# Three edits to a two-layer encoder kernel: early low halves, whole transpose groups, and a (3, 2) projection quota for one tile

## The chip, the cores and the metric

One core of one Trainium2 chip. The time is device microseconds (us) of one execution; lower is better. The kernel is one launch and runs both layers one after the other.

## The reference, cut to what matters

Each of two layers computes `x <- x + RMSNorm(W_out . [A, B, C])` for 1024 prompt rows and 64 sample rows that share the weights. All three branches read `RMSNorm(x)` through one input projection:

```python
proj = einsum('bld,de->ble', rmsnorm(x), w_in)
# A: 4-tap causal convolution, gates, linear recurrence
# B: index scores relu(q_idx . k_idx) summed over 8 heads, top 256 keys per query,
#    softmax over the selected keys only, times v, 4 heads
# C: two softmax maps per head, p0 - lam * p1, times v, RMSNorm per head, 4 heads
mix = einsum('ble,ed->bld', concat([y_a, y_b, y_c]), w_out)
x = x + rmsnorm(mix, norm_post)
```

Attention is block-causal, so a later tile of 128 prompt rows sees more keys. The sample rows see 1024 cached keys and their own 64.

## The kernel before, in words

Rows are split into nine tiles: 0 to 7 are prompt tiles of 128 rows, tile 8 (`SAMPLE`) holds the 64 sample rows. A layer has a **front** and an **attention part**, each written out as a list of steps that every engine walks in the same order, each picking its own steps.

The front (`front()`, L235) begins with transposes of x on TensorE (PE, L1772), and with the index query projection "iq": two halves by three pieces of tokens, six pieces of eight float32 matmuls (L1810; each such matmul is two instructions). Its order is iq pieces, index keys "ik" (L1796), further projections, then the index scores (L1847), with other projections between them, the gates of branch A and the value rows. The projection pieces go around a ring of four PSUM banks. An iq bank is free once ScalarE (ACT) has copied the high half out (L1184, semaphore `high_ready`) and VectorE (DVE) has taken the rounded-off low half, PSUM minus high (L1491, `ring_drained`). DVE walks its own program in order: scale and drain the x tiles (L1432, L1453), then some 20 tiny operations for lambda and the decay constants (L1457 to L1474), then the high and low halves of the cached index keys (L1478, L1480), and then, in a loop over eight ring pieces (L1485), the low halves of iq and ik. Later DVE searches the 256th score of each row by bisection (L1556) and writes the selection masks (L1672 to L1675); only then does it take part in attention.

The attention part (`schedule()`, L145) has 68 **units**, one head (two heads for tile 8) of one tile, in tile order 7, 8, 6, 0, 1, 2, 3, 4, 5. Place n of this order is the number in the steps `("proj", n, q)` and `("rows", n)`. A tile has its C units first (two softmax maps) and then its B units (one map, keys selected). Unit numbers used below: tile 7 is 0 to 7, tile 8 is 8 and 9 (C), 10 and 11 (B), tile 6 is 12 to 19, tile 3 is 44 to 51 (its B, "selected", units 48 to 51), tile 4 is 52 to 59 (C 52 to 55), tile 5 is 60 to 67. In each unit i the list holds: the scores of unit i+1 (`qk`, L1979), DVE's maximum (L1690), ACT's exponential (`exp`, L1344), the combination of the two maps for C (`comb`, L693 to L701), transposes of the map in groups of four 128-key blocks (`tr`, L2010), their evacuation to SBUF (DVE for B, ACT for C: L678, L680), the product with the values of unit i-1 (`pv`, L2032) and its division (`div`, L717 to L731).

All transpose groups share one PSUM bank (`tbank`): PE starts a group only when the one before is evacuated. The 1088 keys of tile 8 make three groups, the third with 64 keys only. The list carries a remainder `rest` for it: the third group of a tile 8 unit is emitted in the following unit, behind that unit's first scores.

Between these steps lies the output projection of a finished tile: `ytr` (L2042) transposes its 512 attention columns, ACT copies them (L1360), and 16 `proj` steps follow (L2077, two instructions each; 8 steps for tile 8). `QUOTA` (L91) says how many a unit of a tile takes, as (C unit, B unit). The last step is followed by ACT's sum of squares (`square`, L1403) and `rows` (DVE L1728 scales the product out of PSUM, GpSimd L1125 adds x, SyncE stores). Places 5 and 6 (tiles 2 and 3) and 7 (tile 4) use the same PSUM banks, so the first `proj` of one waits for the `rows` of the one before. `take()` (L163) holds the next tile's projection back by one unit for that. What is left at the last unit is done behind it, in front of the last tile's own 16 steps.

Of the kernel before, what the change touches and what calls it, by code (L numbers as in the profile page):

```python
# [6 lines left out]
P = 128  # L7
# [16 lines left out]
HI, DI = 8, 32  # L24
# [36 lines left out]
TOKENS = [(0, 384), (384, 384), (768, 320)]  # L61
# [26 lines left out]


FIRST_PROJ = 0  # L90
QUOTA = {0: (2, 3), 1: (2, 2), 2: (2, 2), 3: (3, 3), 4: (2, 2), 5: (2, 2), 6: (2, 1)}  # L91
YTR = 2
NARROW_MIX = (1, 3)
LATE, NEXT_LATE = ORDER[-1], ORDER[-2]
EARLY_X = [[0, 1, 2], [t for t in range(3, NT) if t not in ORDER[-2:]]]
NARROW_END = 7
FIRST_X = 3
ROWS_AT = {-1: [("tm", "bv", 2), ("tm", "bv", 3)], 0: [("tm", "bv", 4)], 1: [("tm", "bv", 5), ("tm", "bv", 6)]}
LAST_ROWS = sum(ROWS_AT.values(), [])

# [44 lines left out]
def schedule():  # L145

    units = ATT
    steps = []
    waiting = []
    finish = []  # L150
    hold = [FIRST[ORDER.index(SAMPLE) + 1] + FIRST_PROJ]
    begun = [0]
    rest = []

    def scores(i):

        if not begun[0] <= i < len(units):
            return []
        begun[0] = i + 1
        return [[("qk", i, m)] + ([("qk2", i, m)] if units[i][0] == SAMPLE else []) + [("exp", i, m)]  # L160
                for m in range(maps_of(i))]

    def take(i, most):  # L163

        new = []
        while waiting and most and i >= hold[0]:
            n, q = waiting.pop(0)
            new.append(("proj", n, q))
            most -= 1
            if q == proj_steps(ORDER[n]) - 1:  # L170
                new.append(("square", n))
                late = 2 if mix_place(n + 1) == mix_place(n) else 1
                finish.append((i + 1, n))
                if late == 2:
                    hold[0] = i + 2
        return new

    steps += sum(scores(0), []) + ROWS_AT[-1]
    for i, (t, kind, h) in enumerate(units):
        nk = -(-width(t) // P)  # L180
        groups = [("tr", i, g) for g in range(-(-nk // 4))]
        rows_now = [("rows", finish.pop(0)[1])] if finish and finish[0][0] <= i else []
        quota = QUOTA.get(t, (0, 0))["CB".index(kind)]
        pv = [("pv", i - 1)] if i else []
        div = [("div", i - 1)] if i else []
        n = NTH[i]
        ytr = []
        if i - FIRST[n] == YTR + 1 and n:
            ytr = [("ytr", n - 1)]
            waiting += [(n - 1, q) for q in range(proj_steps(ORDER[n - 1]))]  # L190
        nxt = scores(i + 1)
        one, two = (nxt + [[], []])[:2]
        own = [("comb", i)]
        plain = kind == "B"
        if len(groups) == 1:
            head = one[:-1] + ytr + one[-1:] + own if plain else own + one[:-1] + ytr + one[-1:]
            soon = rows_now if width(t) > 2 * P else []
            steps += head + take(i, 1) + pv + soon + two + take(i, quota - 1) + groups + div
            steps += [] if soon else rows_now
        elif t == SAMPLE and kind == "C":  # L200
            ahead = scores(i + 2)[0] if len(nxt) == 1 and maps_of(i + 2) == 1 else []
            steps += own + one[:-1] + two[:-1] + rest + ytr + groups[:1] + rows_now + one[-1:] + two[-1:]
            if ahead:
                steps += ahead[:-1] + groups[1:2] + pv + groups[2:] + div + ahead[-1:]
                rest = []
            else:
                steps += pv + groups[1:2] + div
                rest = groups[2:]
        elif t == SAMPLE:
            steps += one[:-1] + rest + ytr + one[-1:] + own + rows_now + two[:-1]  # L210
            steps += groups[:1] + two[-1:] + pv + groups[1:2] + div
            rest = groups[2:]
        elif plain:
            steps += one[:-1] + ytr + one[-1:] + own + take(i, 1) + groups[:1] + two
            steps += take(i, quota - 1) + pv + div + groups[1:] + rows_now
        else:
            steps += own + one[:-1] + rest + ytr + two[:-1] + take(i, 1) + groups[:1] + rows_now + one[-1:] + two[-1:]
            steps += ROWS_AT.get(i, [])
            rest = []
            steps += take(i, quota - 1) + pv + div + groups[1:]  # L220
    last = len(units)
    hold[0] = last
    steps += [("pv", last - 1), ("div", last - 1)]
    while len(waiting) > 2:
        hold[0] = last
        steps += take(last, len(waiting) - 2)
    steps += [("ytr", NT - 1)] + take(last, 2) + [("rows", n) for _, n in finish]
    waiting += [(NT - 1, q) for q in range(proj_steps(ORDER[-1]))]
    hold[0] = last
    new = take(last, 2 * KT)  # L230
    steps += new + [("rows", NT - 1)]
    return steps
# [109 lines left out]
def build(nc, x0, w_in, acst, gate_w, npost, w_out, ckT, kidxT, vcache,  # L342
# [7 lines left out]
    with ctx:  # L350
# [270 lines left out]
        def on_ring(key, w=BANK, r=P):  # L621
            b = RINGBANK[key]
            return ps[0:r, BANK * b:BANK * b + w]
# [7 lines left out]
        def drains_ring(ins, key):  # L631
            return ins.then_inc(ring_drained[RINGBANK[key]], 1)
# [101 lines left out]
        for layer in range(DEPTH):  # L734
# [5 lines left out]
            with nc.Block() as block:  # L740
# [666 lines left out]
                def _(dve):  # L1407
                    steps = [0]

                    def link(ins):  # L1410
                        steps[0] += 1
                        ins.then_inc(dve_step, 1)
                        dve.wait_ge(dve_step, steps[0])
# [23 lines left out]
                    for t in range(NT):  # L1437
# [16 lines left out]
                        if not has_prev and 3 <= t + 1 < NT:  # L1454
                            scale_x(t + 1, t + 2, xt[t + 1])

                    dve.wait_ge(lam_e, 1)  # L1457
                    link(vec.tensor_tensor(lamp, lams[:, 3:4], lams[:, 2:3], ALU.subtract))
                    vec.tensor_tensor(nlam, lamp, cst[:, C_INIT:C_INIT + 1], ALU.subtract).then_inc(lam_ready, 1)
# [20 lines left out]
                    vec.tensor_tensor(ikcs[half, :], ikc[half, :], ikcs[half, :].bitcast(f32), ALU.subtract)\  # L1480
                       .then_inc(kc_low, 1)

                    third = slice(64, 96)
                    n = 0
                    for key in list(RINGJOB)[:2 * len(TOKENS) + 2]:  # L1485
                        _, u, c, p = key
                        n += 1
                        dve.wait_ge(high_ready, n)
                        if u == "iq":
                            c0, cn = TOKENS[p]  # L1490
                            drains_ring(vec.tensor_tensor(iq3[1][:, c, c0:c0 + cn], on_ring(key, cn),  # L1491
                                                          iq3[0][:, c, c0:c0 + cn].bitcast(f32), ALU.subtract), key)
                        else:
                            cols = slice(2 * IKW * p, 2 * IKW * (p + 1))
                            vec.tensor_copy(iks[DI:2 * DI, cols], iks[0:DI, cols].bitcast(f32))
                            link(vec.tensor_tensor(iks[third, cols], ikf[0:DI, cols], iks[0:DI, cols].bitcast(f32),
                                                   ALU.subtract))
                            vec.tensor_copy(iks[96:P, cols], iks[third, cols].bitcast(f32)).then_inc(kn_low, 1)

                    for j in range(AJ):  # L1500
                        vec.memset(ax[j][:, 0:3], 0.0)
# [671 lines left out]
```

## Time and profile before

| what | value |
|---|---|
| three runs | 1584.02, 1585.23, 1580.79 us (median 1584.02) |
| the profiled execution | 1586.94 us |
| its span, first to last instruction | 1585.2 us |
| mean granted TensorE clock | 0.987 |
| PE busy | 1523.2 us (96%) |
| DVE busy | 1140.4 us (72%) |
| ACT busy | 648.3 us (41%) |
| GpSimd (POOL) busy | 371.5 us (23%) |

PE is TensorE's matmul side. "Idle before" is the time for which an engine had nothing to execute before an instruction, with the instruction that ended the wait. A granted clock of 1.00 is TensorE's 2.4 GHz level, 0.50 its 1.2 GHz level; a window's figure is the mean over it. Layer 0 runs to about 793.5 us of the span, layer 1 from there.

### The profile page before, as it was taken

To read this page: it belongs to the slowest core of one execution; us is meant where nothing else is said; L and a number is where in the kernel's file an instruction comes from. 1 tells how busy PE (TensorE), PEld (TensorE's weight loads), DVE (VectorE), ACT (ScalarE), POOL (GpSimd) and SP (SyncE) were. 2 spreads that over 40 slices of the span, in tenths; PEclk is the share of its full clock that TensorE was granted. 3 is DMA by queue.
4 is the path that set the end of the run, shared out by engine and by line. 5 is a ranking of instruction groups with operands and counts; after the bars stand their busy time and mean duration, and the time that the engine had idled before them with its cause. 6 is when DMAs were issued, how large, how long until landed. Compare 5 with 4: busy or idle time off the path is not lost. (4 is left out here: it accounts for less than half of the span.)

```text
span 1585.2 us, 21171 instructions
## 1 busy us (share of the span) xinstructions
PE 1523.2 (96%) x7264; PEld 1026.0 (65%) x7286; DVE 1140.4 (72%) x2482; ACT 648.3 (41%) x1270; POOL 371.5 (23%) x461
## 2 busy tenths in 40 slices
PE   7999999999999899999989999999999999999997
PEld 5566556678877665566556665566788766556664
DVE  5479979998966556666443799899989666565662
ACT  3385760219143333434314757402371433343341
POOL 2000341430001244332310004404200121434221
PEclk9999999999999999999999999999999999999999
DMA  5101001231015112120411200023210341112111
GB/s 189 57 13 42 27 27 27 79 99 49 27 50 207 67 34 67 43 68 11 170 60 57 27 27 27 27 50 97 80 54 1 116 144 66 51 56 68 41 35 40
DMA packets 73114, 98.16 MB, mean 62 GB/s; under 512 B 42736, under 2 KB 61680, under 8 KB 68656
## 3 DMA queue, kind: packets, MB, share of 16 engines
q1 hardware_dynamic: 73008, 96.80, 19.9%
q8 instruction: 59, 0.97, 0.2%
q14 instruction: 47, 0.39, 0.1%
HBM read 65.79 MB, written 18.14 MB: 53 GB/s over the span
## 5 line engine op out<-in xcount | busy, mean ns | idle before, releaser
L1810 PE MATMUL ps<-r_xn,r_w 128*128 128x384 f32 (+1 forms) x1728 | 563.7, 476 | 7.8 <-DVE r_xn L1453 2.7
L1810 PEld LDWEIGHTS ps<-r_xn,r_w 128*128 128x128 f32 x1728 | 325.5, 192 | 198.4 <-issue 24.9
L1556 DVE TENSOR_SCALAR_CACHE_REDUCE r_ix<-r_sc,smi 128x768 bf16<-128x768 f32 (+6 forms) x380 | 342.1, 963 | 2.2
L1344 ACT ACTIVATE r_sc<-ps,sm 128x1024 f32<-128x1024 f32 (+8 forms) x204 | 155.5, 765 | 225.8 <-DVE sm L1690 225.6
L1896 PE MATMUL ps<-r_w,r_xn 128*128 128x256 f32 x1024 | 224.0, 380 | 0.0
L1896 PEld LDWEIGHTS ps<-r_w,r_xn 128*128 128x128 f32 x1024 | 193.8, 190 | 26.8 <-issue 1.0
L1690 DVE TENSOR_REDUCE sm<-ps 128x1 f32<-128x1024 f32 (+8 forms) x204 | 156.2, 786 | 54.5 <-PE ps L1985 20.5
L2032 PEld LDWEIGHTS ps<-r_vg,r_w 128*128 128x128 f32 (+1 forms) x1168 | 147.6, 192 | 53.1 <-issue 33.5
L2032 PE MATMUL ps<-r_vg,r_w 128*128 128x64 f32 (+1 forms) x1168 | 148.3, 271 | 1.3 <-DVE r_w L678 1.2
L2077 PE MATMUL ps<-r_xn,r_ag 128*128 128x512 f32 x256 | 134.2, 623 | 2.6 <-ACT r_vg L1360 2.6
L2077 PE MATMUL ps<-r_xn,r_vg 128*128 128x512 f32 x256 | 131.0, 607 | 0.4 <-DMA r_xn<-w_out 0.2
L2010 PEld LDWEIGHTS ps<-ident,r_sc 128*128 128x128 f32 (+1 forms) x648 | 80.7, 147 | 73.2 <-issue 55.4
L2010 PE MATMUL ps<-ident,r_sc 128*128 128x128 f32 (+1 forms) x648 | 110.6, 281 | 11.2 <-DVE r_w L680 5.3
L1518 DVE SCALAR_TENSOR_TENSOR r_sc<-r_vg,sm,r_sc 128x384 f32<-128x384 f32 (+6 forms) x98 | 97.8, 998 | 27.2 <-ACT r_vg L1252 21.6
L678 DVE COPY r_w<-ps 128x512 f32<-128x512 f32 (+3 forms) x104 | 59.1, 568 | 80.1 <-issue 51.8
L1252 ACT ACTIVATE r_vg<-ps 128x384 f32<-128x384 f32 (+6 forms) x112 | 88.4, 795 | 28.5 <-PE ps L1847 22.7
L678 ACT COPY r_w<-ps 128x512 f32<-128x512 f32 (+3 forms) x104 | 50.6, 486 | 115.4 <-PE ps L2010 114.7
L717 DVE TENSOR_SCALAR r_q<-ps,sm 128x64 f32<-128x64 f32 x128 | 35.9, 281 | 82.0 <-PE ps L2032 81.5
L1306 ACT ACTIVATE r_ix<-r_sc,smi 128x896 bf16<-128x896 f32 (+2 forms) x60 | 67.2, 1120 | 24.5 <-DVE smi L1654 17.4
L700 DVE SCALAR_TENSOR_TENSOR r_sc<-r_sc,sm 128x512 f32<-128x512 f32 (+3 forms) x104 | 67.9, 682 | 2.4
L1847 PE MATMUL ps<-iks,iqs 128*128 128x384 f32 (+3 forms) x160 | 67.7, 494 | 1.5 <-ACT iqs L1234 1.5
L1058 POOL CAST qb_hi<-r_qk 64x256 fp32r<-64x256 f32 x32 | 12.6, 394 | 239.5 <-ACT r_vg L1294 232.6
(256 smaller groups left out, 1868.9 us busy)
## 6 DMA issues: line engine op xcount, KB each, us to landing
r_w<-w_in SPq DMA_DIRECT2D x24, 1024.0 KB, 5.0
r_xn<-w_out SPq DMA_DIRECT2D x4, 2048.0 KB, 7.5
y<-r_res SPq DMA_DIRECT2D x15, 512.0 KB, 2.9
r_vg<-x SPq DMA_DIRECT2D x8, 512.0 KB, 8.6
r_w<-w_in SPq DMA_DIRECT2D x16, 256.0 KB, 5.5
r_xn<-vcache SPq DMA_DIRECT2D x2, 2048.0 KB, 12.5
o_v<-r_vg SPq DMA_DIRECT2D x4, 1024.0 KB, 10.6
r_sc<-x SPq DMA_DIRECT2D x8, 512.0 KB, 4.6
```

The lines of the kernel that those rows point to most:

```text
L678: ins = copy(pT[i % 2][:, k0:k1, 0:r], src[:, 0:k1 - k0, 0:r])
L700: vec.scalar_tensor_tensor(e0, e1, cf, e0, ALU.mult, ALU.add).then_inc(comb_ready, 1)
L1252: drains_x(nc.scalar.activation(dst, src, ACT.Relu, scale=scale), key)
L1344: ins = nc.scalar.activation(ex[2 * (i % 2) + m][0:r, 0:w], on_slot(("qk", i, m), w, r), ACT.Exp, bias=negm[0:r, c:c + 1], accum_out=den[0 ...
L1518: ins = vec.scalar_tensor_tensor(sc[t][0:r, 0:w], src, iw[0:r, t, h:h + 1], sc[t][0:r, 0:w], ALU.mult, ALU.add)
L1556: ins = vec.tensor_scalar(unsel[t][0:rows(t), :], sc[t][0:rows(t), :], b, None, op, ALU.add, accum_out=cnt[0:rows(t), c:c + 1])
L1690: vec.tensor_reduce(negm[0:r, c:c + 1], on_slot(s, w, r), X, ALU.max, negate=True)\
L1810: ins = nc.tensor.matmul(on_ring(key, cn), w[:, k, P * s:P * (s + 1)], xnT[:, k, c0:c0 + cn], start=(k == 0), stop=(k == KT - 1))
L1896: ins = nc.tensor.matmul(on_ring(key)[:, BW * (t - t0):BW * (t - t0 + 1)], xnT[:, k, P * t:P * (t + 1)], w[:, k, :], start=(k == 0), stop= ...
L2010: ins = nc.tensor.transpose(tbank[0:kn, P * (k - 4 * g):P * (k - 4 * g) + r], ex[2 * (i % 2)][0:r, P * k:P * k + kn], ident[0:r, 0:r])
L2032: ins = nc.tensor.matmul(obank[0:r, 0:vals.shape[1]], pT[i % 2][0:kn, k, 0:r], vals, start=(k == 0), stop=(k == nk - 1))
L2077: ins = nc.tensor.matmul(mixb[:, half, :], yk, wo[:, k, BANK * half:BANK * (half + 1)], start=(k == 0), stop=(k == KT - 1))
```

## The change: what it does

Three edits, in both layers.

1. `QUOTA` of tile 3 goes from (3, 3) to (3, 2): its four B units take two projection steps each in place of three.
2. Tile 8's units no longer leave their third transpose group to the next unit if they are B units: all groups of the unit stand in it. New branches for scores two units ahead and for an early start are added to the same place.
3. DVE takes the first four low halves (`EARLY_LOWS = 4`, the iq pieces of the first two token pieces) directly behind the last x tile, before the tiny operations and the cached keys; the other four stay where all eight were.

```diff
-QUOTA = {0: (2, 3), 1: (2, 2), 2: (2, 2), 3: (3, 3), 4: (2, 2), 5: (2, 2), 6: (2, 1)}
+QUOTA = {0: (2, 3), 1: (2, 2), 2: (2, 2), 3: (3, 2), 4: (2, 2), 5: (2, 2), 6: (2, 1)}
+EARLY_LOWS = 4
         elif t == SAMPLE:
-            steps += one[:-1] + rest + ytr + one[-1:] + own + rows_now + two[:-1]
-            steps += groups[:1] + two[-1:] + pv + groups[1:2] + div
-            rest = groups[2:]
+            ahead = []
+            if i + 2 < len(units) and maps_of(i + 1) == maps_of(i + 2) == 1:
+                ahead = scores(i + 2)[0]
+            early = i == FIRST[n]
+            steps += one[:-1] + ytr + ([] if early else one[-1:]) + own + rows_now + two[:-1]
+            if ahead and len(ahead) == 3:
+                steps += groups[:1] + (one[-1:] if early else []) + ahead[:1] + groups[1:2] + ahead[1:2] + groups[2:] + pv + ahead[2:] + div
+            elif ahead:
+                steps += groups[:1] + ahead[:1] + groups[1:2] + pv + groups[2:] + ahead[1:] + div
+            else:
+                steps += groups[:1] + two[-1:] + pv + groups[1:] + div
         else:
-            steps += own + one[:-1] + rest + ytr + two[:-1] + take(i, 1) + groups[:1] + rows_now + one[-1:] + two[-1:]
+            steps += own + one[:-1] + ytr + two[:-1] + take(i, 1) + groups[:1] + rows_now + one[-1:] + two[-1:]
...
+                    def lows(first, last):
+                        for n in range(first, last):
+                            key = list(RINGJOB)[n]
+                            dve.wait_ge(high_ready, n + 1)
...
+                    lows(0, EARLY_LOWS)
                     dve.wait_ge(lam_e, 1)
...
-                    for key in list(RINGJOB)[:2 * len(TOKENS) + 2]:
...
+                    lows(EARLY_LOWS, 2 * len(TOKENS) + 2)
```

The lists that come out, for PE, around tile 8's B units (10 and 11) and tile 6's first unit, layer by layer the same:

```
before: tr10.0 pv9 tr10.1 | qk12.0 tr10.2 ytr0 qk12.1 tr11.0 pv10 tr11.1 | qk13 tr11.2 proj0.0 tr12.0 proj0.1 pv11
after:  tr10.0 pv9 tr10.1 tr10.2 | qk12.0 ytr0 qk12.1 tr11.0 pv10 tr11.1 tr11.2 | qk13 proj0.0 tr12.0 proj0.1 pv11
```

The projection of tile 2 (place 5) ended in unit 53 and ends in unit 55; `rows5` stood in unit 54 and stands in unit 56. Tile 3's (place 6) covered units 55 to 62 and covers 57 to 64; `rows6` moves from unit 63 to 65. Tile 4's (place 7) had 8 of its 16 steps in units 64 to 67 and now has 4 in units 66 and 67; 12 in place of 8 steps are left behind unit 67.

## Rows read from the trace of the kernel before

**Rows 1.** The page: its first line.

```profile
span 1585.2 us, 21171 instructions
```

**Rows 2.** Waits of PE: releaser, us in total, times, longest.

```profile
PE ps L2010 <- DVE r_w L680: 5.3, 2, 2.7
PE ps L2042 <- DVE r_w L680: 4.2, 2, 2.1
...
PE ps L1810 <- issue: 2.6, 1, 2.6
...
PE ps L1810 <- DVE iq_lo L1491: 2.6, 1, 2.6
```

**Rows 3.** Timeline, front of layer 0: start, us, engine, line, instruction, idle before.

```profile
39.05 0.15 DVE L1458 TENSOR_TENSOR sm<-sm 128x1 f32<-128x1 f32 x1
...
42.51 0.49 ACT L1184 ACTIVATE iq_hi<-ps 128x384 fp32r<-128x384 f32 x1 [5.51 <-PE ps L1810]
...
44.41 1.95 DVE L1491 TENSOR_TENSOR iq_lo<-ps,iq_hi 128x384 fp32r<-128x384 f32 x4
```

**Rows 4.** Windows: bounds, length, PE busy, granted clock, DMA share, GB/s.

```profile
42.00:52.00 10.00, 7.40 (x22) 0.83 0.00 0
827.00:837.00 10.00, 7.45 (x22) 0.83 0.00 0
516.00:536.00 20.00, 15.26 (x82) 0.83 0.06 14
1302.00:1322.00 20.00, 16.70 (x87) 0.83 0.14 35
704.00:714.00 10.00, 8.37 (x36) 0.83 0.36 121
1486.00:1498.00 12.00, 10.01 (x45) 0.72 0.31 102
470.00:480.00 10.00, 8.75 (x63) 1.00 1.00 303
```

**Rows 5.** Timeline, PE at the B units of tile 8, layer 0.

```profile
514.11 0.66 PE L2010 MATMUL ps<-ident,r_sc 128*128 128x128 f32 x4
...
518.12 0.66 PE L2042 MATMUL ps<-ident,r_q 128*128 128x128 f32 x4 [2.09 <-DVE r_w L680]
...
529.62 1.02 PE L2010 MATMUL ps<-ident,r_sc 128*128 128x128 f32 x4 [2.65 <-DVE r_w L680]
```

**Rows 6.** Timeline, DVE at the same place.

```profile
514.80 0.69 DVE L678 COPY r_w<-ps 128x512 f32<-128x512 f32 x1 [1.89 <-PE ps L2010]
...
517.79 0.27 DVE L680 COPY r_w<-ps 64x128 f32<-64x128 f32 x1
```

**Rows 7.** Timeline, DVE and PE at tile 4, units 54 and 55, layer 0.

```profile
703.52 1.27 DVE L1728 SCALAR_TENSOR_TENSOR r_res<-ps,sm,r_ix 128x1024 f32<-128x1024 f32 x1
...
701.83 0.63 PE L2010 MATMUL ps<-ident,r_sc 128*128 128x128 f32 x4 [0.38 <-DVE r_sc L700]
...
704.85 0.47 PE L1979 MATMUL ps<-kst_b,qb_hi 128*128 128x512 f32 x1 [1.21 <-DVE r_res L1728]
...
707.25 2.04 PE L2077 MATMUL ps<-r_xn,r_ag 128*128 128x512 f32 x2 [0.78 <-ACT r_vg L1360]
```

**Rows 8.** Timeline, PE at unit 63, layer 0.

```profile
748.94 0.66 PE L2010 MATMUL ps<-ident,r_sc 128*128 128x128 f32 x4 [0.69 <-ACT r_vg L1360]
```

**Rows 9.** Timeline, DVE and PE in a B unit of tile 4.

```profile
712.26 0.48 PE L1979 MATMUL ps<-kst_b,qb_hi 128*128 128x512 f32 x1
...
713.48 0.82 DVE L1690 TENSOR_REDUCE sm<-ps 128x1 f32<-128x640 f32 x1 [0.50 <-PE ps L1985]
...
716.60 0.48 PE L1979 MATMUL ps<-kst_b,qb_hi 128*128 128x512 f32 x1
```

**Rows 10.** The chain that ended last, behind unit 67 of layer 1: start, us, what.

```profile
1562.04 15.47 PE ps L2077 x36
```

**Rows 11.** Timeline, DVE's first instruction of the attention part, layer 0.

```profile
445.02 1.23 DVE L1690 TENSOR_REDUCE sm<-ps 128x1 f32<-128x1024 f32 x1 [1.54 <-PE ps L1992]
```

More of the change, by code:

```diff
@@ L216, in schedule @@
         else:
-            steps += own + one[:-1] + rest + ytr + two[:-1] + take(i, 1) + groups[:1] + rows_now + one[-1:] + two[-1:]
+            steps += own + one[:-1] + ytr + two[:-1] + take(i, 1) + groups[:1] + rows_now + one[-1:] + two[-1:]
             steps += ROWS_AT.get(i, [])
-            rest = []
             steps += take(i, quota - 1) + pv + div + groups[1:]
@@ L1455, in _ @@
                             scale_x(t + 1, t + 2, xt[t + 1])
+                    third = slice(64, 96)
+                    def lows(first, last):
+                        for n in range(first, last):
+                            key = list(RINGJOB)[n]
+                            _, u, c, p = key
+                            dve.wait_ge(high_ready, n + 1)
+                            if u == "iq":
+                                c0, cn = TOKENS[p]
+                                drains_ring(vec.tensor_tensor(iq3[1][:, c, c0:c0 + cn], on_ring(key, cn),
+                                                              iq3[0][:, c, c0:c0 + cn].bitcast(f32), ALU.subtract), key)
+                            else:
+                                cols = slice(2 * IKW * p, 2 * IKW * (p + 1))
+                                vec.tensor_copy(iks[DI:2 * DI, cols], iks[0:DI, cols].bitcast(f32))
+                                link(vec.tensor_tensor(iks[third, cols], ikf[0:DI, cols], iks[0:DI, cols].bitcast(f32),
+                                                       ALU.subtract))
+                                vec.tensor_copy(iks[96:P, cols], iks[third, cols].bitcast(f32)).then_inc(kn_low, 1)
+                    lows(0, EARLY_LOWS)
                     dve.wait_ge(lam_e, 1)
@@ L1481, in _ @@
                        .then_inc(kc_low, 1)
-                    third = slice(64, 96)
-                    n = 0
-                    for key in list(RINGJOB)[:2 * len(TOKENS) + 2]:
[L1486 to L1498, printed above, removed]
+                    lows(EARLY_LOWS, 2 * len(TOKENS) + 2)
                     for j in range(AJ):
```

## The prediction

> **What bounds the kernel now.** I read the page first, then PE's waits, then the timeline around each long wait, then windows of the granted clock. The profiled execution took 1586.94 us, its span 1585.2 [rows 1]; so it stands 2.9 us above the median of the runs, 1584.02, and 1.7 us lie around the span. What I take off is taken off both alike. PE is busy for 1523.2 us of the span, no other engine beyond 1140.4; PE is the bound, and its time can only fall where it waits or where its clock is at the lower level. The waits of PE [rows 2] show few long ones: 2.6 us in each layer in front of the third iq piece pair (L1810), 2.1 and 2.65 us in each layer at L2042 and L2010, all behind DVE. A last group stands at tile 4 [rows 7]: 0.38, 1.21 and 0.78 us within 6 us. The reader should then see in the windows [rows 4] that each of these places also has a granted clock below 1: 0.83 over 10 us is 1.7 us of clock time lost, and each such window starts with one of these waits. So a wait costs its length and, at five places in layer 0 and its twins in layer 1, some 1.7 us more.
>
> **Early low halves.** DVE ends the x tiles at 39.05 and goes through the tiny operations and the cached keys until 44.41; only then it frees the first ring bank (L1491, 0.49 us each), while PE stood from 42.47, for 2.6 us [rows 2, 3]. After the change three of the four high halves are there at 39.05, so the first bank is free at 39.6, 2.9 us before PE asks. The fourth low half needs ACT's copy that ends at 43.0 [rows 3]; DVE waits for it, and its 5.3 us of other work moves to 43.5 to 48.9. Who waits for that: the index scores, which need the cached keys at 68; and the ring bank of the fifth piece, whose high half came at 51.3 even before. Cost zero, covered by two whole iq pieces; without the cover it would be 5.3 us. Gain: 2.60 + 2.55 us of wait, and the clock at 42 to 52 and 827 to 837, 0.17 x 10 us each [rows 4]: 3.4. **Sum 8.55.** Bounds: 5.15 if the clock falls nevertheless, 8.55 if not.
>
> Does that reach the end? PE's front leads to DVE's search. DVE begins attention after a wait of 1.54 us for PE [rows 11]; its search starts from the index scores and moves with them. PE itself waits for DVE nowhere there. I let it pass whole.
>
> **Whole groups in tile 8's B units.** No instruction is added; the third group and its evacuation (0.27 us) move. The new branches never run with this tile order: they ask for two more one-map units behind, and unit 12 has two maps. Before, `ytr0` came right behind the third group, whose evacuation stood in DVE's queue behind the division of unit 9 and a maximum, at 517.79 [rows 6]: a wait of 2.09 [rows 5]. The second time the evacuation stood behind a division, a combination and a maximum: 2.65. After: the third group follows the second with only that one's evacuation between. The second ends at 514.77, its evacuation at 515.49 [rows 5, 6]: a wait of 0.75 to 0.8, once in unit 10 and once in unit 11. `ytr0` then has unit 12's scores in front and finds the bank empty. `tr12.0` waits for the combination, which now comes behind a small evacuation and a division only: by DVE's durations about 4.1 us behind the end of pv10, where PE arrives at 3.7; I take 0.5. New waits per layer 0.8 + 0.8 + 0.5 = 2.1 against 4.74: 2.6 gained. On clock, the windows 516 to 536 and 1302 to 1322 lose 0.17 x 20 = 3.4 us each [rows 4]. Waits of 0.34 and 0.91 us within 3 us left the clock at 1.00 in the window from 470 to 480; the new ones are smaller or further apart, so I take all of it back. **Sum 2 x (2.6 + 3.4) = 12.0.** Bounds: the clock stays lost, 5.2; the waits vanish, 16.2. Two edges lose something: DVE's maxima come 0.5 us later, still ahead of pv11; and the second half of w_out is fetched behind unit 11's product, so it moves with it.
>
> Transposes themselves run at both levels here: four take 0.66 us at 514.11 and 1.02 at 529.62, behind the long wait [rows 5]. The Trainium skill has a rule that speaks against this part: its page "TensorE: Matmul & The Clock Gate", section "Part 4: PE-mode transpose", says that the full clock "doesn't engage" for transposes. By it, two groups in a row with a wait between them would bring the low level back at these four places, and the sum here would be 5.2. The 0.66 speaks against the rule as it stands; whether the clock falls sooner among transposes the trace does not separate.
>
> **The quota of tile 3.** A step is two instructions of 0.43 us [rows 10], 0.86. Four units give up one each; tile 2's last three groups of two now lie in units 53 to 55, and 4 steps more, 3.4 us, stand behind unit 67. PE's work is the same; the sum is waits and clock. Removed per layer: in unit 54 two steps go between the scores and `tr54.0` and cover the 0.38 and most of the 1.21 (DVE and ACT need 4.5 us for such a unit, PE with two steps 4.7); in unit 55 a step covers ACT's copy of `ytr6`, 0.78 [rows 7]; in unit 63 the same, 0.69 [rows 8]. 3.06 us. Clock: 1.7 at 704 to 714, and 0.28 x 12 = 3.4 at 1486 to 1498, where 0.4 of it lies on a wait already counted [rows 4]: 4.7.
>
> Added: units 56 and 65 have no steps. A B unit of tile 4 takes 4.34 us with two steps [rows 9], so 2.6 without. DVE needs, from its start, 1.2 until the scores are there, 0.82 for the maximum, 0.69 for the first evacuation, some 1.1 for division and second evacuation, and then `rows5`, 1.27 [rows 7, 9]: 5.1. The second group waits 0.35 for the first evacuation, and proj6.0, due at 2.6 + 0.35 + 1.0 of scores, waits for `rows5` 1.05. At unit 65 the same gives about 0.2 and 0.8. Together 2.4 per layer. Zero if PE's stream is slower than I lay it out; 3.5 if GpSimd's root comes late. POOL's addition of `rows5` comes behind its head norm, later by some 4 us; its readers, the store and `rows6`, are 30 us away. SyncE's queue has `rows5` now behind tile 5's query copies instead of before; both are early. Tile 3's own units stay PE's: with two steps they hold 3.7 us against less than 2 of DVE. In layer 0 the longer remainder moves the last tile's chain together with the steps behind it. **Sum 6.1 + 4.7 - 4.8 = 6.0.**
>
> Total 8.55 + 12.0 + 6.0 = 26.5. I take off 1 for edges (unit 54's 0.15, unit 10's division later by 0.6). So 25.5: 1561.4 for the profiled execution, and **1558.5** against the median.
>
> **Rivals.**
>
> A. *The new waits lower the clock.* Places: tile 8's four (two in each layer) and units 56/57, 65/66 in both layers, eight in all, 1.7 us each. For: 1.21 and 0.78 us sufficed in layer 0, and in layer 1 the level was low already right behind the 1.21 [rows 4, 7]; units 56/57 have 1.4 us of waits in 2 us. Against: 470 to 480. With half of the eight, +6.8: 1565. (The Trainium skill's rule on transposes, above, would give it at the tile 8 places.)
> B. *DVE takes the front's gain back.* If the search does not move with PE, PE may gain only the 1.54 us [rows 11] of the 4.3 a layer: +5.5, 1564. Against: every wait of DVE in the front is for ACT, POOL or PE, which all move.
> C. *Slower.* TensorE falls to 1.2 GHz at every wait left or new in tiles 8, 6, 4 and 5, ten a layer or more. Price 1.7 us each; it turns the result from the 15th place on (25.5 / 1.7), and 20 would give 1592. Against: ten waits of 0.3 to 0.5 us leave 1.00 now.
> D. *The part on tile 3 does nothing*, its waits for `rows` being as long as the ones removed: 1564.5; it is a case of A by size.
>
> **How the numbers follow.** Forecast as laid out: 0.60, with 1554 to 1562 of its own (the added waits of tile 4 vanish, -4.8; one or two falls of the clock, +3.4). A 0.23, B 0.06, D 0.06, C 0.02, and 0.03 for no change by something unseen. The range runs from 1553 to 1570: it holds A to seven places, B and D. About 0.3% (4.8 us) is what a measurement of this kernel can tell from no change. Faster by more 0.95, within 0.03, slower 0.02.
>
> **What would show it.** The waits of L1810 for `iq_lo` and of L2042 and L2010 for L680 gone; in tile 8 two waits of L2010 for L678 of 0.8 us in each layer; windows at the five places at 1.00; units 54 and 55 without 1.21 and 0.78; two new waits of L2077 for DVE's L1728, near 1.0 and 0.8 us; a remainder behind unit 67 longer by 3.4 us. I am wrong if the clock is low at tile 8 still, if PE meets DVE where attention begins, or if L2077 waits for L1728 for over 2 us.

## The result, and the profile after

The changed kernel took **1560.19 us** in the median of four executions (1555.93 to 1562.50), the kernel before 1583.86 beside it on the same chip (1580.79 to 1585.23): a ratio of **0.985**, 95% interval 0.9825 to 0.9876. The prediction was 1558.5 with a range of 1553 to 1570, so the size came out. Whether the reasons did is what the rest is about: one of its two kinds of gain was too large, the other too small.

The page of the profiled execution (1560.33 us; mean granted clock 0.997, before 0.987), its span and each engine's busy time with its share of the span:

```profile
span 1558.5 us, 21195 instructions
PE 1510.0 (97%) x7286; PEld 1017.4 (65%) x7286; DVE 1132.5 (73%) x2482; ACT 649.5 (42%) x1270; POOL 370.7 (24%) x461
```

The span is 26.7 us shorter than in [rows 1]. PE's idle times, summed over its timeline, fell from 52.1 to 38.8 us; PE's busy time fell by 13.2 (from 1523.2), although its instructions are the same. That second half is clock: the same matmuls took less time at the higher level. The line numbers of the kernel have moved: L1810 is now L1823, L2010 L2023, L2042 L2055, L1979 L1992, L2077 L2090, L1728 L1741, L1491 L1475, L678 and L680 L686 and L688.

Waits of PE after (releaser, us in total, times, longest), against [rows 2]:

```profile
PE ps L2023 <- DVE r_w L686: 3.5, 6, 0.8
...
PE ps L2090 <- DVE r_res L1741: 2.7, 4, 0.7
...
PE ps L1823 <- issue: 1.4, 1, 1.4
PE ps L1823 <- DVE r_xn L1461: 1.3, 1, 1.3
```

The four large groups of [rows 2] are gone: nothing waits for the third group's evacuation on DVE or for the low halves. The two L1823 lines left are the waits for the first x tiles at the head of each layer, which were there before.

The front of layer 0 (start, us, engine, line, instruction, idle before), against [rows 3]:

```profile
37.46 12.75 PE L1823 MATMUL ps<-r_xn,r_w 128*128 128x384 f32 x44
38.17 1.47 DVE L1475 TENSOR_TENSOR iq_lo<-ps,iq_hi 128x384 fp32r<-128x384 f32 x3
42.16 0.56 DVE L1475 TENSOR_TENSOR iq_lo<-ps,iq_hi 128x384 fp32r<-128x384 f32 x1 [2.51 <-ACT iq_hi L1192]
```

PE goes through all iq pieces without a stop. DVE pays 2.51 us of its own time for the fourth low half, and nobody waits for DVE there.

PE at tile 8's B units (the first three in layer 0, the others in layer 1), against [rows 5]:

```profile
510.22 0.30 PE L2023 MATMUL ps<-ident,r_sc 128*64 128x128 f32 x1 [0.78 <-DVE r_w L686]
...
517.34 0.30 PE L2023 MATMUL ps<-ident,r_sc 128*64 128x128 f32 x1 [0.78 <-DVE r_w L686]
...
520.26 0.63 PE L2023 MATMUL ps<-ident,r_sc 128*128 128x128 f32 x4 [0.47 <-DVE r_sc L708]
...
1280.42 0.30 PE L2023 MATMUL ps<-ident,r_sc 128*64 128x128 f32 x1 [0.78 <-DVE r_w L686]
1289.10 0.30 PE L2023 MATMUL ps<-ident,r_sc 128*64 128x128 f32 x1 [0.79 <-DVE r_w L686]
...
1304.05 1.12 PE L2090 MATMUL ps<-r_xn,r_vg 128*128 128x512 f32 x2 [0.75 <-DMA r_xn<-w_out]
```

The waits of 2.09 and 2.65 us have become 0.78, 0.78 and 0.47. In layer 1 the second half of w_out is now 0.75 us late; before, PE waited 0.24 us for it, in layer 0.

The windows that answer to [rows 4] (bounds, length, PE busy, granted clock, DMA share, GB/s):

```profile
36.00:56.00 20.00, 20.00 (x107) 1.00 0.15 54
800.00:830.00 30.00, 30.00 (x156) 1.00 0.11 36
505.00:525.00 20.00, 17.61 (x116) 1.00 0.28 104
1274.00:1296.00 22.00, 19.61 (x121) 0.92 0.28 102
685.00:705.00 20.00, 18.48 (x116) 1.00 0.05 14
1450.00:1475.00 25.00, 22.90 (x139) 1.00 0.04 12
```

Five of the six places are back at 2.4 GHz. The sixth, tile 8 in layer 1, still falls to 1.2 GHz once: 0.08 x 22, about 1.7 us. That is one of the signs by which the prediction said that it would be wrong.

### The profile page after: what moved, and what is told of

The parts are those of the page before. It is cut to its first block, busy times and chain, and to the rows that moved or that the text cites. A ratio compares the mean times of both kernels' runs of the same rounds, so it can differ in the third digit from the quotient of the medians.

```text
span 1558.5 us, 21195 instructions
## 1 busy us (share of the span) xinstructions
PE 1510.0 (97%) x7286; PEld 1017.4 (65%) x7286; DVE 1132.5 (73%) x2482; ACT 649.5 (42%) x1270; POOL 370.7 (24%) x461
## 4 chain that ended last, share of the span: by engine, by line
PE 45%; DVE 2%; issue 1%; ACT 1%; DMA 1%; POOL 0%; ACTq 0%; DVEq 0%; POOLq 0%
PE ps L1823 17%; PE ps L1909 7%; PE ps L2090 7%; PE ps L2045 4%; PE ps L1992 3%; PE ps L2023 2%; PE ps L1860 1%; ACT r_sc L1352 1%; PE ps L1888 1%; DMA r_xn<-w_out 1%; DVE sm L1703 1%; PE ps L2085 1%; PE ps L1902 0%; PE ps L1809 0%; PE ps L1785 0%
## 5 line engine op out<-in xcount | busy, mean ns | idle before, releaser
L1823 PE MATMUL ps<-r_xn,r_w 128*128 128x384 f32 (+1 forms) x1728 | 558.1, 472 | 2.7 <-issue 1.4
L1823 PEld LDWEIGHTS ps<-r_xn,r_w 128*128 128x128 f32 x1728 | 322.6, 190 | 190.5 <-issue 17.7
L2090 PE MATMUL ps<-r_xn,r_ag 128*128 128x512 f32 x256 | 131.0, 607 | 2.7 <-DVE r_res L1741 2.7
L2090 PE MATMUL ps<-r_xn,r_vg 128*128 128x512 f32 x256 | 130.3, 607 | 0.9 <-DMA r_xn<-w_out 0.8
L2023 PEld LDWEIGHTS ps<-ident,r_sc 128*128 128x128 f32 (+1 forms) x648 | 79.3, 145 | 69.3 <-issue 53.4
L2023 PE MATMUL ps<-ident,r_sc 128*128 128x128 f32 (+1 forms) x648 | 109.3, 278 | 7.9 <-DVE r_w L686 3.5
L686 DVE COPY r_w<-ps 128x512 f32<-128x512 f32 (+3 forms) x104 | 59.1, 568 | 72.8 <-issue 46.7
L686 ACT COPY r_w<-ps 128x512 f32<-128x512 f32 (+3 forms) x104 | 50.6, 486 | 104.2 <-PE ps L2023 103.5
L1066 POOL CAST qb_hi<-r_qk 64x256 fp32r<-64x256 f32 x32 | 12.7, 396 | 236.7 <-ACT r_vg L1302 232.6
```

The source lines that it names most:

```text
L686: ins = copy(pT[i % 2][:, k0:k1, 0:r], src[:, 0:k1 - k0, 0:r])
L1823: ins = nc.tensor.matmul(on_ring(key, cn), w[:, k, P * s:P * (s + 1)], xnT[:, k, c0:c0 + cn], start=(k == 0), stop=(k == KT - 1))
L2023: ins = nc.tensor.transpose(tbank[0:kn, P * (k - 4 * g):P * (k - 4 * g) + r], ex[2 * (i % 2)][0:r, P * k:P * k + kn], ident[0:r, 0:r])
L2090: ins = nc.tensor.matmul(mixb[:, half, :], yk, wo[:, k, BANK * half:BANK * (half + 1)], start=(k == 0), stop=(k == KT - 1))
```

## The experiments

**How the table was made.** Each execution comes with its span and mean granted clock c. (1 - c) x span is called the clock cost here: what the lower level would cost if PE worked all through it (one stretch at 1.2 GHz, a "fall", is 0.17 x 10 us = 1.7 us; a stretch twice as long counts as two). c x span is the rest, with all waits in it. c is rounded to 0.001, 1.6 us in one execution, so only means over the executions are used.

The split is rough. In 15 executions of the kernel before, the three at c = 0.993 had spans of 1577.7, 1578.9 and 1578.9 us, the four at 0.986 and 0.987 spans from 1584.2 to 1586.9: 7.0 us of span for 10.0 us of clock cost, so a part of the clock cost costs nothing. One such part can be seen: in every profile the level also falls behind PE's last instruction. In the kernel before, PE is busy for 0.00 us from 1577.50 to 1585.20, and the granted clock of that window is 0.73, some 2 us of clock cost for nothing. The 2.5 and 1.9 us of v_act and v_best below are about what this end alone gives. "PE idle", summed over the profiled execution, is an independent reading of the waits. Each ratio is to the kernel before, run beside it on the same chip.

| kernel | median us | ratio, 95% interval | clock cost us | rest us | PE idle us |
|---|---|---|---|---|---|
| before (15 executions) | 1583.51 | 1 | 16.5 | 1565.5 | 52.1 |
| the change | 1560.19 | 0.985 (0.9825 to 0.9876) | 5.5 | 1552.4 | 38.8 |
| e_lows | 1578.95 | 0.9964 (0.9949 to 0.9978) | 17.0 | 1559.4 | 47.4 |
| e_groups | 1570.24 | 0.992 (0.9904 to 0.9936) | 8.6 | 1560.6 | 47.3 |
| e_quota | 1575.27 | 0.995 (0.9935 to 0.9965) | 12.9 | 1561.0 | 48.5 |
| a_nolows | 1566.26 | 0.9891 (0.9871 to 0.991) | 8.1 | 1556.4 | 43.6 |
| a_divfirst | 1557.35 | 0.9836 (0.9813 to 0.9858) | 3.5 | 1552.1 | 37.4 |
| a_low2 | 1559.74 | 0.9851 (0.9822 to 0.9881) | 5.9 | 1552.0 | 39.4 |
| a_low8 | 1566.73 | 0.9904 (0.988 to 0.9929) | 9.8 | 1556.5 | 46.7 |
| v_both | 1562.78 | 0.9863 (0.9843 to 0.9883) | 8.6 | 1552.1 | 39.2 |
| v_act | 1556.02 | 0.9824 (0.9804 to 0.9844) | 2.5 | 1551.6 | 38.6 |
| v_best | 1553.85 | 0.9813 (0.9792 to 0.9833) | 1.9 | 1550.3 | 37.0 |
| v_q | 1553.81 | 0.982 (0.98 to 0.9839) | 4.7 | 1548.1 | 34.4 |

Falls of the clock in the profiled execution, up to 1.7 us each, layer 0 + layer 1. Those at the head of a layer (none or one each, whatever the kernel) and at the very end are left out:

| kernel | front, behind the third iq pair | tile 8 and the unit behind it | tile 4 |
|---|---|---|---|
| before | 1 + 1 | 2 + 2 | 1 + 2 |
| e_lows | 0 + 0 | 2 + 3 | 0 + 1 |
| e_lows, second profile | 0 + 0 | 2 + 2 | 2 + 3 |
| e_groups | 1 + 1 | 0 + 0 | 0 + 0 |
| e_quota | 1 + 1 | 2 + 2 | 0 + 0 |
| a_nolows | 1 + 1 | 0 + 0 | 0 + 0 |
| the change | 0 + 0 | 0 + 1 | 0 + 0 |
| a_divfirst | 0 + 0 | 0 + 2 | 0 + 0 |
| a_low2 | 0 + 0 | 2 + 2 | 0 + 0 |
| a_low8 | 0 + 0 | 0 + 2 | 0 + 0 |
| v_both | 0 + 0 | 2 + 2 | 0 + 0 |
| v_act, v_best, v_q | 0 + 0 | 0 + 0 | 0 + 0 |

Two profiles have further falls, which none of these columns counts: a_low8 one in layer 0 and two in layer 1 at the cached keys, and one in tile 6 of layer 1 behind a wait of 1.14 us for w_out; v_q one in layer 1's front behind a wait of 0.75 us for ACT, where v_best has the same wait and no fall.

**One part at a time.** The kernel before with one of the three edits each. First the early low halves:

```diff
+EARLY_LOWS = 4
+                    lows(0, EARLY_LOWS)
                     dve.wait_ge(lam_e, 1)
...
+                    lows(EARLY_LOWS, 2 * len(TOKENS) + 2)
```

> The kernel before with the early low halves alone. The theory of the prediction: 2.60 + 2.55 us of PE's waits for the third iq pair go, and the granted clock at 42 to 52 and 827 to 837 is 1.00, 0.17 x 10 us each: 8.55 us less than before (ratio 0.9946). Rival (DVE takes it back where attention begins): 3 us less. Rival (the clock falls nevertheless): 5.2 us less. The waits of tiles 8 and 4 stay as they were.

Measured: 0.9964, which is 5.7 us less (3.5 to 8.1). The rest fell by 6.1 us, about the 5.15 of waits; the clock cost did not fall at all (17.0 for 16.5). The front itself shows the whole gain. Here PE is in e_groups, whose front is that of before, and then in e_lows, from the first iq matmul to the first product with the index keys; neither has a fall at the head of the layer:

```profile
15.36 1.53 PE L1818 MATMUL ps<-r_xn,r_w 128*128 128x384 f32 x4 [1.36 <-issue]
...
70.31 0.60 PE L1855 MATMUL ps<-iks,iqs 128*128 128x384 f32 x2 [0.74 <-ACT iqs L1242]
```

```profile
14.17 1.21 PE L1816 MATMUL ps<-r_xn,r_w 128*128 128x384 f32 x3 [1.36 <-DVE r_xn L1454]
...
64.60 0.60 PE L1853 MATMUL ps<-iks,iqs 128*128 128x384 f32 x2 [0.74 <-ACT iqs L1235]
```

That is 55.0 and 50.4 us, 4.5 less; in layer 1 it is 54.5 and 50.1. So the front gave 8.9 us in these profiles, and the shortfall of the whole lies behind it. A second profile of the same kernel was taken for the places of the falls:

> The kernel before with the early low halves alone, looked at once more, for the places at which the clock falls. If the part removes the falls in the front: none at 40 to 50 nor at 805 to 835, as in the first look, whatever the others do. If the number of falls elsewhere is chance: another count than in the first look (about two at tile 8 in layer 0, three in layer 1, none and one at tile 4). Time between 1573 and 1581 us, 1.7 us for each fall.

It took 1579.06 us. Windows of this second profile:

```profile
40.00:50.00 10.00, 10.00 (x37) 1.00 0.00 0
805.00:835.00 30.00, 29.87 (x143) 1.00 0.14 43
698.00:708.00 10.00, 8.01 (x32) 0.66 0.33 111
1474.00:1490.00 16.00, 13.34 (x62) 0.68 0.25 81
```

The front behind the third iq pair is at the full level in both profiles, as the prediction had it. But tile 4 has five falls here, where the kernel before has three and the first profile one. The waits there are those of before; in layer 0:

```profile
696.26 0.50 PE L1985 MATMUL ps<-kst_c,qc_hi 64*128 64x512 f32 x2 [0.29 <-ACT r_sc L1345]
...
697.77 0.63 PE L2016 MATMUL ps<-ident,r_sc 128*128 128x128 f32 x4 [0.38 <-DVE r_sc L701]
...
700.79 0.64 PE L1985 MATMUL ps<-kst_b,qb_hi 128*128 128x512 f32 x1 [1.22 <-DVE r_res L1734]
...
704.39 2.05 PE L2083 MATMUL ps<-r_xn,r_ag 128*128 128x512 f32 x2 [0.78 <-ACT r_vg L1361]
```

Then the whole groups alone:

```diff
-            steps += groups[:1] + two[-1:] + pv + groups[1:2] + div
-            rest = groups[2:]
+                steps += groups[:1] + two[-1:] + pv + groups[1:] + div
```

> The kernel before with the whole transpose groups of tile 8's B units alone. The theory of the prediction: 2.6 us of wait and 3.4 us of clock in each layer, 12.0 us less (ratio 0.9924). If the clock falls once behind the new waits of 0.78 us in layer 1, as in the changed kernel's profile, 10.3 less. Rival (transposes with waits between them hold the clock at the lower level in both layers): 5.2 us less.

Measured: 0.992, 12.7 us less; clock cost 7.9 us less, the rest 4.9. Tile 8 is at 1.00 in both layers. This kernel still has the quota of before, and tile 4 has the same four waits as the profile above, yet its windows read:

```profile
40.00:50.00 10.00, 7.41 (x21) 0.83 0.00 0
...
505.00:525.00 20.00, 17.83 (x116) 1.00 0.32 116
1280.00:1300.00 20.00, 17.73 (x115) 1.00 0.32 116
690.00:715.00 25.00, 21.97 (x133) 1.00 0.16 53
1465.00:1490.00 25.00, 21.96 (x140) 1.00 0.17 54
```

```profile
693.86 0.51 PE L1987 MATMUL ps<-kst_c,qc_hi 64*128 64x512 f32 x2 [0.29 <-ACT r_sc L1352]
695.36 0.63 PE L2018 MATMUL ps<-ident,r_sc 128*128 128x128 f32 x4 [0.38 <-DVE r_sc L708]
698.38 0.47 PE L1987 MATMUL ps<-kst_b,qb_hi 128*128 128x512 f32 x1 [1.22 <-DVE r_res L1736]
700.79 1.10 PE L2085 MATMUL ps<-r_xn,r_ag 128*128 128x512 f32 x2 [0.78 <-ACT r_vg L1368]
```

Waits of 0.29, 0.38, 1.22 and 0.78 us, once with no fall and once with two: what a wait of about a microsecond does to the clock differs from execution to execution. Of the waits compared here only those above 2 us, in front and at tile 8, had a fall in every profile.

Then the quota:

```diff
-QUOTA = {... 3: (3, 3), ...}
+QUOTA = {... 3: (3, 2), ...}
```

> The kernel before with the quota of tile 3 at (3, 2) alone. The theory of the prediction: 6.1 us of waits and 4.7 us of clock go, 4.8 us of new waits come: 6.0 less (ratio 0.9962). The changed kernel's trace has the new waits at 0.62 and 0.71 us in place of 1.4 and 1.0, so about 8 less by that. Rival (the waits for the rows are as long as those removed): no difference. Windows of tile 4 at clock 1.00 in both layers by the first, below 1 by the rival.

Measured: 0.995, 7.9 us less; clock cost 3.6 less, the rest 4.5 (PE idle 3.6). Tile 4 is at 1.00. The rival (no difference) is out. The three ratios alone add up to 5.7 + 12.7 + 7.9 = 26.3 us; the change has 23.8 (0.015 x 1583.9). They are additive within their intervals, each some 2 us to either side. The quota's share without the clock can also be read between e_groups and a_nolows, which differ in the quota alone and have no fall at tile 4: the rest is 4.2 us less and PE idle 3.7.

**The low halves once more, the other way round.** The changed kernel with EARLY_LOWS at 0, 2 and 8 (one line each):

> The changed kernel without the early low halves (all eight where they stood before). The prediction's term: 8.55 us more than the changed kernel (ratio to before 0.990). What the run with this part alone showed, 5.7 us with its clock mean no higher than that of before: 5.2 to 5.7 us more (0.988). If the falls of the clock in the front are real and come at every execution: two more falls than the changed kernel in the windows of the profile, at 40 to 50 and 805 to 835.

Without early low halves the ratio is 0.9891, 6.5 us more than the change (0.0041 x 1583.9). The two waits of 2.6 us and the two falls are back; the profile's PE idle is 4.8 us more. The two intervals together leave 5 us to either side of this 6.5, so it confirms the term and says little of its size; the 5.7 of e_lows is the better figure, and its interval ends at 8.1.

> The changed kernel with two early low halves in place of four. Theory: only the ring banks of the first two pieces are asked for in the 5.3 us of DVE's other work, so two early ones do all: the changed kernel's time within 1 us (ratio to before 0.985), PE without a wait from 37 to 50 us, and no fall of the clock there. Rival (the third and fourth matter): the wait returns in front of the index keys, 1 us or more a layer.

Two are enough: 0.9851, and no fall from 36 to 56 us. Its windows at tile 8 show what the chance of a fall means; the waits are 0.79, 0.78 and 0.48 us, the change's own:

```profile
505.00:525.00 20.00, 17.61 (x92) 0.83 0.27 103
1275.00:1295.00 20.00, 17.63 (x98) 0.83 0.33 118
```

> The changed kernel with all eight low halves early, so that DVE's tiny operations and cached keys, 5.3 us, stand behind the index keys' low halves and begin at 60.8 in place of 42.6. If the prediction's cost of zero for the moved work holds because two iq pieces cover it: the cover is gone here and PE waits for the cached keys where the index scores begin (65 to 68 us): up to 5.3 us a layer, about 1 us to 3 us each, so 2 to 6 us more than the changed kernel. Rival (that work has far more room than the prediction gave it): no difference.

Measured: 0.9904, 8.6 us more than the change (0.0054 x 1583.9), a little beyond the estimate of 2 to 6, whose upper end the intervals do not exclude. PE in layer 0:

```profile
67.68 0.40 PE L1847 MATMUL ps<-iq_hi,selh 32*128 32x256 f32 x4 [2.82 <-DVE ikcs L1508]
69.40 0.98 PE L1860 MATMUL ps<-iks,iqs 128*128 128x384 f32 x2 [1.20 <-ACT iqs L1242]
```

The cached keys (L1508) are what PE waits for once their cover is gone: 2.8 us in each layer, 0.45 more at the wait for ACT, and falls of the clock behind. So the cost of zero in the prediction was a matter of cover, as it said: with four the cover holds, with eight it does not.

**Which half of the edit at tile 8 pays.** PE does the third group ahead of the next scores, and DVE evacuates it ahead of the division. Here DVE does the division first and PE's list is the change's:

```diff
-                steps += groups[:1] + two[-1:] + pv + groups[1:] + div
+                steps += groups[:1] + two[-1:] + pv + groups[1:2] + div + groups[2:]
```

> The changed kernel with DVE's division ahead of the evacuation of the third group in tile 8's B units; PE's own order is the changed kernel's. It tells PE's half of the edit (the group ahead of the next scores) from DVE's half (the small evacuation ahead of the division). If PE's place does it: the transposes of tile 7's output wait some 0.4 us per layer and nothing else changes: 1 us more than the changed kernel (0.9855). If DVE's order does it: the waits of 2.1 and 2.65 us return and with them falls of the clock at tile 8: 8 us more or beyond (0.990).

Measured: 0.9836, no slower than the change (the intervals overlap). PE's place does it; the rival had 0.990 and the long waits, and neither came. DVE in unit 11, first in the changed kernel, where it stands for 0.39 us:

```profile
517.67 0.28 DVE L688 COPY r_w<-ps 64x128 f32<-64x128 f32 x1 [0.39 <-PE ps L2023]
...
519.36 1.28 DVE L708 SCALAR_TENSOR_TENSOR r_sc<-r_sc,sm 128x512 f32<-128x512 f32 x2
```

and with the division first, where it doesn't:

```profile
517.33 0.29 DVE L728 TENSOR_SCALAR r_w<-ps,sm 64x64 f32<-64x64 f32 x1
...
518.19 0.28 DVE L688 COPY r_w<-ps 64x128 f32<-64x128 f32 x1
...
518.89 1.28 DVE L708 SCALAR_TENSOR_TENSOR r_sc<-r_sc,sm 128x512 f32<-128x512 f32 x2
```

The division fills the time in which PE transposes, the combination starts 0.47 us sooner, and PE's wait of 0.47 for it is gone. The expected 0.4 us at the transposes of tile 7's output did not come. By PE's waits DVE's half of the edit was a small loss, 0.47 us a layer; in the time of the whole it cannot be told from nothing.

**Toward a faster version.** Two moves: the third group behind the next scores on PE but ahead of the division on DVE, and in tiles 4 and 5 the first projection step behind rows after the unit's first transposes instead of ahead of them.

```diff
-                steps += groups[:1] + two[-1:] + pv + groups[1:] + div
+                steps += groups[:1] + two[-1:] + pv + groups[1:2]
+                rest = groups[2:] + div
...
-            steps += one[:-1] + ytr + one[-1:] + own + take(i, 1) + groups[:1] + two
-            steps += take(i, quota - 1) + pv + div + groups[1:] + rows_now
+            m = waiting[0][0] if waiting and waiting[0][1] == 0 else 0
+            fresh = m > 0 and mix_place(m) == mix_place(m - 1)
+            steps += one[:-1] + ytr + one[-1:] + own + ([] if fresh else take(i, 1)) + groups[:1] + two
+            steps += take(i, quota if fresh else quota - 1) + pv + div + groups[1:] + rows_now
```

> The changed kernel with two moves. In tile 8's B units PE does the next scores between the second and the third transpose group, as before the change, but DVE still evacuates the third group ahead of the division and the maximum. In tile 4 and 5 the first projection step behind the rows of the place before comes behind the unit's first transpose group instead of ahead of it. The theory that a wait costs its length plus some 1.7 us where the clock falls: the two waits of 0.78 us per layer go, 0.2 to 0.6 us come at the transposes of tile 7's output, the waits of 0.62 and 0.71 us go; 1.0 + 0.6 us a layer and 1.7 us for the clock fall in layer 1: some 5 us less than the changed kernel, 1555 us (ratio to before 0.982). Rival (the waits only move to the next instruction, as DVE's stream is what PE waits for): within 1 us of the changed kernel, 0.985.

A miss: 0.9863, no faster than the change. (In this kernel the division of unit 10 comes behind the combination of unit 12 and takes that unit's sum, so its result is wrong there. The instructions are the same in number and size, and only its times are used.) The scores carry DVE's maximum with them, so it stands ahead of the third evacuation after all:

```profile
512.21 1.09 DVE L1708 TENSOR_REDUCE sm<-ps 128x1 f32<-128x896 f32 x1 [0.48 <-PE ps L2010]
513.22 0.27 DVE L693 COPY r_w<-ps 64x128 f32<-64x128 f32 x1
...
513.55 1.11 PE L2060 MATMUL ps<-ident,r_q 128*128 128x128 f32 x4 [1.27 <-DVE r_w L693]
```

The 1.11 us for four transposes is the 1.2 GHz level: the falls were back. The answer is to take the small evacuation off DVE. v_act has the list of before at tile 8 and ACT for the third group; v_best adds the move of the projection step above.

```diff
-                        elif s[0] == "tr" and ATT[s[1]][1] == "C":
+                        elif s[0] == "tr" and (ATT[s[1]][1] == "C" or s[2] == 2):
...
-                            if ATT[s[1]][1] == "B":
+                            if ATT[s[1]][1] == "B" and s[2] < 2:
```

> The changed kernel with the ACT evacuation and the old place of the third group alone. Theory: 0.7 us of waits a layer and one fall of the clock, 3.1 us less than the changed kernel (ratio to before 0.983). Rival (the waits only move): the changed kernel's time, 0.985.

> The changed kernel with the third transpose group of tile 8's B units behind the next unit's first scores again, evacuated by ACT (idle there) in place of DVE, and with the first projection step of places 6 and 7 behind the unit's first transpose group. Theory (PE's waits plus 1.7 us for each fall of the clock are all there is): per layer the two waits of 0.78 us go, some 0.35 us come at the transposes of tile 7's output and the wait for the combination grows by some 0.5; 0.9 us of 1.35 go at the two waits for the rows: 1.6 us a layer, 3.2, and less one fall of the clock, 1.7: 5 us less than the changed kernel (ratio to before 0.982). Rival (DVE's chain of division, combination and maximum is what PE waits for at tile 8, so only the place of the wait moves): 2 us less (0.984).

Measured: v_act 0.9824, 4.1 us less than the change, with intervals that overlap; v_best **0.9813**, 1553.85 us (1553.22 to 1555.13), every execution below the fastest of the change. PE at tile 8 in v_act:

```profile
510.89 0.66 PE L2048 MATMUL ps<-ident,r_q 128*128 128x128 f32 x4 [0.35 <-ACT r_w L681]
519.40 0.63 PE L2016 MATMUL ps<-ident,r_sc 128*128 128x128 f32 x4 [1.25 <-DVE r_sc L701]
```

Here the rival was nearly right about the waits and the theory about the time. At tile 8 the waits are 0.35 + 1.25 in place of 0.78 + 0.78 + 0.47, 0.4 us less a layer, and other places give that back: PE idle is 38.6 for 38.8. What fell is the clock cost, 2.5 for 5.5 us, and no profile of a kernel with this edit (v_act, v_best, v_q: six places) has a fall at tile 8. Why one wait of 1.25 us spares the clock that two of 0.78 sometimes lose is not settled; v_both had its two falls right behind one of 1.27. The moved projection step left 0.9 of the 2.7 us of waits for rows, and v_best's PE idle is 1.6 less than v_act's.

Last, v_best with the quotas of tiles 3 and 4 at (2, 2) and (3, 2):

> The kernel v_best with one more edit: the quota of tile 3 at (2, 2) and that of tile 4 at (3, 2), so that tile 4's two-map units take three steps. Theory (at tile 4 PE is short of work by what its waits show): v_best's waits there for ACT's exponentials, 0.63, 0.51, 0.29 and 0.45 us in each layer, go, 1.9 a layer; tile 3's two-map units, now with two steps, may wait 0.5 in exchange: 2 to 4 us less than v_best, about 1551 us (ratio to before 0.9795). Rival (three steps make tile 4's waits go but tile 3's last two-map units and unit 55, with one step left, wait as long): v_best's time, 0.981.

0.982, the time of v_best, as the rival had it, though by another way: the waits did go (PE idle 34.4 for 37.0, the rest 1548.1 for 1550.3), and the clock cost rose from 1.9 to 4.7, of which the profile shows one fall, in layer 1's front, where the edit changes nothing. With four executions each, whether that rise is chance stays open.

## Why the prediction was right, and where it was off

**The bound.** PE bound the kernel before and after, and nothing was given back at another engine. Rival B (DVE takes the front's gain back) is out: PE began attention 5.4 us earlier in layer 0, where the profile of before also had a fall at the head of the layer.

**Early low halves, 8.55 predicted, 5.7 measured alone (3.5 to 8.1).** In the front the term held. The waits (5.15) went, and so did the two falls, in all nine profiles of kernels with two or four early; all four profiles with none early have both. The front became shorter by 4.5 and 4.4 us. The cost of zero held, and a_low8 gave its price without cover. What failed is the step from there to the whole: "I let it pass whole", with "the clock at 42 to 52 and 827 to 837" as 3.4 us of gain. Two falls fewer should bring the clock cost from 16.5 to some 13; in ten executions it was 17.0, and each of the two means is good to about 1 us. So falls came elsewhere: 6 and 9 at tiles 8 and 4 in the two profiles, beside the 7 of before. That is hard to put down to chance alone. Whether an earlier front makes falls behind it likelier is not shown, and in the other setting (a_nolows, 2.6 us more clock cost than the change) nothing of the kind is seen. The cause stays open.

**Whole groups, 12.0 predicted, 12.7 measured alone.** Waits of 0.8, 0.8 and 0.5 were predicted, 0.78, 0.78 and 0.47 came. "I take all of it back" was too much for the clock: six profiles have these waits (a_divfirst without the 0.47), and their twelve places show 0, 1, 0, 0, 0, 0, 2, 2, 0, 2, 0, 2 falls (the change, e_groups, a_nolows, a_low2, a_low8, a_divfirst, two places each), nine in all, against at least two in every place with the waits of before. That is 1.5 falls an execution, 2.6 of the 6.8 us. This is rival A at the tile 8 places, and it is the likely reason why the change's four executions spread from 1555.93 to 1562.50, with granted clocks from 0.998 to 0.994; where the clock fell in the three without a profile is not on record. The Trainium skill's page "TensorE: Matmul & The Clock Gate", section "Part 4: PE-mode transpose", says that the full clock "doesn't engage" for transposes. As it stands the runs contradict it: four took 0.66 us behind waits of 0.35, and the level stayed full in seven of the twelve places. But at these transposes it did fall behind waits of at most 0.8 us, and at tile 4, where the new waits for `rows` are 0.6 and 0.7, it never did. The wait of 0.5 for the combination was priced rightly but taken as a price of the edit. It comes from DVE's half alone, as a_divfirst showed, and the gain needs only PE's half.

**The quota, 6.0 predicted, 7.9 measured alone.** The mis-sized term is "Together 2.4 per layer" for the added waits. Unit 56 in the changed kernel:

```profile
697.66 0.69 DVE L686 COPY r_w<-ps 128x512 f32<-128x512 f32 x1
...
698.41 0.33 PE L2023 MATMUL ps<-ident,r_sc 128*128 128x128 f32 x1 [0.20 <-DVE r_w L686]
...
698.98 1.28 DVE L1741 SCALAR_TENSOR_TENSOR r_res<-ps,sm,r_ix 128x1024 f32<-128x1024 f32 x1
...
700.31 1.12 PE L2090 MATMUL ps<-r_xn,r_ag 128*128 128x512 f32 x2 [0.62 <-DVE r_res L1741]
```

Between the first evacuation's end, at 697.66 + 0.69 = 698.35, and `rows` lie 0.63 us, not "some 1.1 for division and second evacuation". (By its own figures the wait of 1.05 comes to 1.13.) The waits are 0.20 and 0.62 in place of 0.35 and 1.05, and at unit 66 0.71 in place of 1.0: 0.87 less a layer, 1.7 in all. It brings the predicted net of 1.3 us of waits to 3.0, beside the 3.6 that PE's idle time fell by. The clock term held (3.6 measured, 4.7 predicted), and none of the ten profiles with tile 3's quota cut shows a fall at tile 4.

**The sum.** By the table the waits gave 13.1 us (10.65 predicted, the 1 for edges off) and the clock 11.0 (14.9); PE idle, which fell by 13.3, bears the first figure out. The two errors, +2.5 and -3.9, leave 1.4 of 25.5, so the closeness of the total is in part luck. The profiled execution of before was an unlucky one: its clock cost is 20.6 us by its mean of 0.987, where 15 executions have 16.5 in the mean. The prediction noted its 2.9 us above the median as an offset and did not see that they were most likely clock time, which a sum over its windows counts as gain.

## What to carry to other kernels

Here a stop of the bounding engine cost its length each time and the clock behind it only with a probability, which one profile does not show: count falls over several executions, and price them by the mean. When the order of two engines is one list, ask for each moved step which engine's half of the move pays; the other half may cost. A gain that is read in one place is not yet a gain of the whole: compare the stretch and the total, as e_lows shows. A small piece of work on a busy engine that gates the bound is best given to one that stands idle there.

## What the runs showed of the hardware

The granted clock did not repeat from execution to execution. With the same waits of 0.29, 0.38, 1.22 and 0.78 us the level stayed at 2.4 GHz in one execution (e_groups) and fell twice to 1.2 in another (e_lows, second profile); the kernel before spread from 0.986 to 0.993 in its mean, 9 us in its span. The kernels with the fewest falls also spread least: 9.2 us (1579.53 to 1588.68) in 15 executions of before, 1.9 us in four of v_best. A low level while PE has nothing to do costs nothing: the last 7.70 us of the kernel before stand at 0.73 and hold no PE instruction.
